# Three transposes of the compressed branch moved from the compression stage into the in-projection

## What is computed

```
proj = h @ w_in
chunks = kv_pad[:, :, :2].reshape(b, n_chunks, 16, 2, KV_HEADS, HEAD_DIM)
pa = einsum('bnlrkd,rlde->bnrke', chunks, w1[:, :16])
pb = einsum('bnlrkd,rlde->bnrke', chunks, w1[:, 16:])
hidden = gelu(pa[:, :-1] + pb[:, 1:] + pos_bias)
out = einsum('bnrke,ref->bnrkf', hidden, w2)      # r = 0: keys, r = 1: values
```

## Time and profile before

| what | value |
| --- | --- |
| median of 3 runs | 2507.48 us (2502.42 to 2513.97) |
| profiled execution | 2507.33 us, span 2505.7 us |
| mean granted TensorE clock | 0.939 of full |
| PE busy | 2372.7 us (95%) |
| DVE busy | 1292.7 us (52%) |
| ACT busy | 647.6 us (26%) |
| POOL busy | 188.6 us (8%) |
| in-projection of layer 0 ends, compression begins | at about 170 us |
| the same in layer 3 | at about 1958 us |

### The profile page before, as it was taken

How to read it: one execution, slowest core, us unless ns; L and a number is a source line. 1 busy time by engine, 2 the same in 40 slices (tenths; PEclk the granted TensorE clock), 3 DMA queues, 4 the chain that set the end, 5 groups by cost and what they waited for, 6 DMA issues and landing times. The chain is left out here.

```text
span 2505.7 us, 45103 instructions
## 1 busy us (share of the span) xinstructions
PE 2372.7 (95%) x18686; PEld 2002.1 (80%) x18686; DVE 1292.7 (52%) x2074; ACT 647.6 (26%) x1603; POOL 188.6 (8%) x346
## 2 busy tenths in 40 slices
PE   8999998899999888999999999999999998989998
PEld 6568765699987767999888856799996787648998
DVE  2237674366552383665443277076551686526565
ACT  1101372211022342210232195122011115522200
POOL 0245000000000010000000011000005520000000
PEclk8999898999999978999999857999999898999999
DMA  9886727956644318566534244666563675393440
GB/s 347 273 251 166 227 81 244 354 209 225 243 154 153 101 50 295 202 241 231 179 133 138 71 118 146 238 255 227 212 214 110 179 223 163 96 308 135 169 168 18
DMA packets 295776, 472.72 MB, mean 189 GB/s; under 512 B 22428, under 2 KB 120749, under 8 KB 295094
## 3 DMA queue, kind: packets, MB, share of 16 engines
q1 hardware_dynamic: 265714, 432.98, 50.7%
q0 software_dynamic: 10240, 20.99, 3.1%
q10 hardware_dynamic: 19618, 15.86, 2.1%
HBM read 448.72 MB, written 38.04 MB: 194 GB/s over the span
## 5 line engine op out<-in xcount | busy, mean ns | idle before, releaser
L632 PE MATMUL PS<-hT,ring 128*128 128x132 f32 x2048 | 249.6, 277 | 6.8 <-DVE hT L757 4.2
L632 PEld LDWEIGHTS PS<-hT,ring 128*128 128x128 f32 x2048 | 238.3, 190 | 12.0 <-issue 11.3
L632 PE MATMUL PS<-mT,arena 128*128 128x132 f32 x1536 | 184.6, 276 | 0.0
L632 PEld LDWEIGHTS PS<-mT,arena 128*128 128x128 f32 x1536 | 178.7, 190 | 0.0
L2688 PE MATMUL PS<-hT,ring 128*128 128x264 f32 x768 | 172.7, 386 | 0.1
L2688 PEld LDWEIGHTS PS<-hT,ring 128*128 128x128 f32 x768 | 145.1, 190 | 24.9 <-issue 0.4
L769 DVE TENSOR_TENSOR arena<-arena,PS 128x264 f32<-128x264 f32 x224 | 89.6, 426 | 131.1 <-PE PS L632 129.9
L948 POOL DMA_DIRECT2D arena<-in_cache_nsa_kv x192 | 97.4, 507 | 493.2 <-issue 438.8
L632 PE MATMUL PS<-arena,ring 128*128 128x132 f32 x1024 | 126.9, 277 | 0.0
L632 PE MATMUL PS<-hT,arena 128*128 128x132 f32 x1024 | 125.7, 276 | 0.0
L632 PE MATMUL PS<-mT,ring 128*128 128x132 f32 x1024 | 125.7, 276 | 0.0
(11 more groups left out here) (502 smaller groups left out, 4346.0 us busy)
## 6 DMA issues: line engine op xcount, KB each, us to landing
arena<-in_w_ada SPq DMA_DIRECT2D x36, 2048.0 KB, 12.1
ring<-in_w_mlp_in SPq DMA_DIRECT2D x32, 2048.0 KB, 8.9
ring<-in_w_mlp_out SPq DMA_DIRECT2D x32, 2048.0 KB, 8.3
ring<-in_w_ada SPq DMA_DIRECT2D x12, 2048.0 KB, 18.3
ring<-in_ssd_w_in SPq DMA_DIRECT2D x12, 2048.0 KB, 8.0
ring<-in_nsa_w_in SPq DMA_DIRECT2D x10, 2048.0 KB, 9.0
ring<-in_cache_nsa_kv SPq DMA_DIRECT2D x128, 128.0 KB, 3.7
ring<-in_hg_w_in SPq DMA_DIRECT2D x8, 2048.0 KB, 7.9
```

Of the source, the lines that this page charges most:

```text
L632: ins = nc.tensor.matmul(PS[:, bank, at:at + HALF], lhs[:, k, p * 128:(p + 1) * 128], rhs[:, k, :], start=opens and k == 0, stop=closes an ...
```

## The change

Transposes 1, 2 and 3 of the first cached round leave the compression stage. DVE makes them in the in-projection of each NSA layer, into the same place in the arena. In layer 0 DVE first waits for both stores of the bias matrices, and in both layers for all of POOL's pages of group 0; the three stand ahead of `move(10)` in layer 0 and ahead of the key copies. Transpose 0 stays where it was, since its quarter holds `wg`. In the compression stage the counts of the semaphore `turned` are adapted, and the differences 1, 2 and 3 no longer wait for it.

```diff
+        def rows_of(buffer, r, j):
+            return buffer.rearrange("p (y t) (r k h d) -> p t r h k y d", t=2, r=2, k=KV, h=2)[:, j // 2, r, j % 2]
+        def columns_of(x, j):
+            return x[:, j, :].rearrange("p (o b y) -> p y o b", o=4, b=2)
+        EARLY = (1, 2, 3)
...
             G = compress_buffers(P)
+            tokens = Place(P.at)(4, 1024)
             wg = P(8, 48)
...
                 if first:
+                    v.wait_ge(bias_kept.sem, bias_kept.at(32))
+                v.wait_ge(fetched_pool[0].sem, fetched_pool[0].at(1024))
+                for j in EARLY:
+                    turned.on(nc.vector.transpose(columns_of(tokens, j), rows_of(G[0], 0, j)))
+                if first:
                     move(10)
                     add(10)
                     move(11)
...
+            def turned_to(m):
+                return turned.at(1 if m in (0, *EARLY) else m + 1 - len(EARLY))
...
-                        sp.wait_ge(turned.sem, turned.at(8 * (g - 1)))
+                        sp.wait_ge(turned.sem, turned_to(8 * (g - 1) - 1))
...
                         j = m % 4
-                        v.wait_ge(turned.sem, turned.at(m + 1))
+                        if m not in EARLY:
+                            v.wait_ge(turned.sem, turned_to(m))
                         differed.on(nc.vector.tensor_tensor(delta[:, j, :].rearrange("p (a n) -> p a n", a=2), shifted(j),
...
                     turn(0)
                     sum_weights(0)
-                    turn(1)
                     position(0)
                     for m in range(1, last):
                         n, j = divmod(m, 4)
-                        if m + 1 < last:
+                        if m + 1 < last and m + 1 not in EARLY:
                             turn(m + 1)
```

More of the change, by code:

```diff
@@ L1285, in compressed @@
                 out_taken.on(ins)
[L1287 to L1295, removed]
             def shifted(j):
@@ L1317, in _ @@
                     for g in (2, 3):
-                        sp.wait_ge(turned.sem, turned.at(8 * (g - 1)))
+                        sp.wait_ge(turned.sem, turned_to(8 * (g - 1) - 1))
                         quarter_pages(sp, mybir.EngineType.SP, fetched, L, g, G, 0)
                     sp.wait_ge(bias_near.sem, bias_near.at(32))
-                    sp.wait_ge(turned.sem, turned.at(24))
+                    sp.wait_ge(turned.sem, turned_to(23))
                     src = kv_p[L, 0].rearrange("(c i t) r k d -> i c t (r k d)", i=4, t=2)
@@ L1332, in _ @@
                         if g > 1:
-                            gp.wait_ge(turned.sem, turned.at(8 * (g - 1)))
+                            gp.wait_ge(turned.sem, turned_to(8 * (g - 1) - 1))
                         quarter_pages(gp, mybir.EngineType.Pool, fetched_pool, L, g, G, 1)
@@ L1428, in _ @@
                                 else:
-                                    pe.wait_ge(turned.sem, turned.at(4 * n + j + 1))
+                                    pe.wait_ge(turned.sem, turned_to(4 * n + j))
                                 product_made.on(cached_product(n, j))
                             else:
-                                pe.wait_ge(turned.sem, turned.at(4 * n + j + 1))
+                                pe.wait_ge(turned.sem, turned_to(4 * n + j))
                                 product_made.on(prompt_product(n, j))
@@ L1460, in turn @@
                         if n < cached:
-                            ins = nc.vector.transpose(columns_of(j), rows_of(G[g % 2], r, j))
+                            ins = nc.vector.transpose(columns_of(x, j), rows_of(G[g % 2], r, j))
                         else:
```

## The result

| | before | changed |
| --- | --- | --- |
| median | 2506.43 us (20 runs) | 2512.70 us (20 runs) |
| spread | 2497.66 to 2515.81 | 2505.43 to 2523.45 |
| ratio | | 1.0025, 95% interval 1.0014 to 1.0036 |

The changed kernel is 6.3 us slower by the medians. It is a small loss, but it is clear of zero. The forecast was 2513.4 us, +6.0.

The account below looks back on a forecast made before the run. PE bounds the kernel, with layer 0's in-projection held by the load of unit 11. Late pages add 5.9 + 0.1 = +6.0 us there, the other parts 0: 2513.4 us forecast, range 2505 to 2520.

Parts of the forecast that it names:

- Landing of the pages: Layer 0's in-projection: POOL's last page starts at 153.17, lands 8.4 us later at 161.57, and ends DVE's waits.
- What stands behind the wait: Layer 0: `move(10)` queues behind DVE's wait, so PE stands at `turn(10)` until 167.35; unit 11's product starts +5.9 us.
- The product at the lower clock: Layer 0, product of unit 11: 3.62 us at clock 0.50, at most 0.2 more after longer idling; 0.1 taken.
- Zero in layer 3's in-projection: Three added transposes there cost 0, since DVE's idle time leaves 17 us of cover.
- Zero in the compression: Both layers: three transposes less save DVE some 5.4 us but bring PE 0; bounds -5.4 per layer and 0.
- The prediction's own sign of being wrong: The compression shrinking by over 2 us from start to end would refute the zero there.
- the wait of 2.5 us: Layer 0's compression: PE's 2.50 us wait at 229.83 for group 2's pages shifts with the stage and stays.
- DVE's lead is worth nothing: Compression, both layers: PE never waits for a moved transpose, so DVE being further ahead brings 0.
- A: Rival, layer 0: pages land before 155.7, transposes hide in idle time, 2507.5 us; chance 0.14 including in-between values.
- point of decision: Rival A's one deciding place: whether POOL's last page in layer 0 lands before 155.7.
- C: Rival: clock stays low longer, key transposes +2.2, first compression product +3.9, 2.5 given back; 2517 us; chance 0.12.
- B: Rival: differences pace PE in rounds 0 and 1, so both layers give up to 5.4 us; 2502.7; chance 0.06.

Follow-up runs that it names:

- layer 0 only: Changed kernel with transposes 1 to 3 early in layer 0 alone, layer 3 as before: 2512.89 us, ratio 1.0028.
- shared pages: Earlier page issue, and POOL issues a quarter of SP's group 1 pages: changed kernel 2499.11 us, 0.9976; kernel before 2497.60 us, 0.9971.
- without constants: Pages issued earlier and split with POOL, PE's ten opening matmuls on constants omitted: transposes moved 2503.01 us, 0.9980; not moved 2497.82 us, 0.9961.
- earlier pages: POOL issues group 0's second half behind the sixth unit, not the eighth: changed kernel 2501.23 us, 0.9981; kernel before 2503.80 us, 0.9990.

## Why the prediction was right

*Landing of the pages* (161.57, 7.3 us behind the gates' start): 7.18 measured, ended by the pages as said. It was read off the transfer's own row and not off layer 3's 2.2 us, which would have given zero.

*What stands behind the wait*: `turn(10)` at 12.73 us behind the gates' start (13.1 forecast), product of unit 11 at 13.14 (13.3), idle time 8.18 (8.5). Shown by doubling the work (+6.43) and by moving the wait two instructions on (-5.1). One of the reasons given for the landing was read with a wrong label: the shares of 52.2% and 49.8% are those of 158 to 159 us and not of 155 to 160, where it was 49.3% for the pages and 53.5% for the weights. The argument stands by either.

*The product at the lower clock*: 3.64 us against 3.62; I had given it 0.1 more and it took nothing. What I missed is the instruction behind it. The key transposes took 2.49 us and not 2.16, since the clock was still low. The sum came out by small errors that cancel, which is luck: the product starts 5.73 us later and not 5.9, the product takes 0.1 less than allowed, and the key transposes take 0.33 more. The prediction also says that the clock fell in the idle time before the product of unit 11. The trace of the kernel before has 1.00 for that idle time (159.1 to 161.6 us); the clock fell at about 161.8, when the product had begun.

*Zero in layer 3's in-projection*: shown, with 17.9 us of cover where 17 were forecast, and by the 47.28 us that stay.

*Zero in the compression*: right to within what was measured. Over the profiled executions with pages unshared, the six compressions without moved transposes average 123.98 us (122.62 to 124.65) and the ten with them 123.37 (122.27 to 124.09). 0.6 us a layer may be there, but the spread of one kernel's two layers is larger. The prediction's own sign of being wrong, a compression over 2 us shorter, did come in layer 3 (124.49 to 122.37). It does not speak against the zero, since layer 3 of the kernel "layer 0 only", where nothing is moved, has 122.62. The rows give the reason: the compression before waits 2.33 us in round 3, and PE then takes 4.38 us from the product behind the wait to the start of round 4; the changed kernel waits 1.31 and the other 1.73, and both take 2.70.

The forecast that the wait of 2.5 us would stay was off: it was 1.64 in layer 0 and 1.31 in layer 3 (2.50 and 2.33 before). In layer 0 an earlier landing, 56.2 us behind the start of the stage and not 56.8, gives 0.5 of it, and PE coming 0.35 later to round 2 the rest. In layer 3 it is the landing alone (56.0 and not 56.9). Why the pages landed earlier stays open. The reason given, that pages and PE's own work and not DVE pace the stage, is shown by the shared pages (1.4 to 4.6 us a layer off) and by the equal lengths without constants. "DVE's lead is worth nothing" is true of the length of the stage; PE's round 0 gains half a microsecond from it without the constants, and PE then waits that much longer for pages.

*The rivals*: A did not come true, by the very row that spoke against it, but its point of decision held. With pages landed before the bias store the cost vanished. That the weights of unit 11 would then be on time as well was no part of it. Of C a small part came: 0.33 us of the 2.2 on the key transposes, and 0.34 on the first product of layer 0's compression (its position term of round 1 starts 16.67 us behind the start of the stage, 16.33 before), which the wait for group 2 took back. B is answered above, at the kernels without constants.

## What to carry to other kernels

Work moved into another engine's idle time costs nothing only where the data is there at that moment. Look up when its last transfer lands, and put the wait behind every instruction that someone else waits for; here two instructions made five of six microseconds. Before moving work off an engine, look for one wait on it. A margin of half a microsecond is no wait, and making it six brought the length of this stage nothing; where it did turn into a wait, the wait was as small as the margin, and the next transfer swallowed it. The gain lay in the transfers: a few pages out of the way of the weights, and a fairer split of the issuing between two queues, without the moved transposes (0.9971), or with the constants left out too (0.9961). The intervals of these two overlap, so no run here says which is the better.

## What the runs showed of the hardware

The granted clock can fall while PE is busy. In the kernel before with earlier pages PE never idled from 150 to 162 us, and yet (windows: us, busy and count of PE, PEld, DVE, ACT, POOL, then PEclk, DMA share, GB/s):

```profile
153.00:156.00 3.00, 3.00 (x37) 2.80 (x29) 0.29 (x1) 1.02 (x1) 0.00 (x0) 1.00 0.80 314
156.00:158.00 2.00, 2.00 (x25) 1.95 (x24) 0.00 (x0) 0.00 (x0) 0.00 (x0) 0.76 0.92 306
158.00:160.00 2.00, 2.00 (x33) 1.53 (x34) 0.20 (x1) 0.33 (x2) 0.00 (x0) 0.50 0.10 34
```

It fell to 0.50, 1.2 GHz, in the gates, whose 48 instructions have 48 columns each. They took 5.06 us there and 4.55 where it did not fall, and the product of unit 11 2.83 against 1.95 in the changed kernel with earlier pages. That is 1.4 of the 1.5 us between 12.93 and 11.40. It is not the transposes that decide it. Of the six kernels with earlier pages it fell in the gates in three (5.06 us unmoved, and with shared pages 5.13 unmoved and 5.24 moved), and not in the other three (moved, and the two without constants). In the changed kernel it fell while PE idled, and was at 0.50 until 169 us, with the product of unit 11 under way since 165.83:

```profile
160.00:163.00 3.00, 0.00 (x0) 0.00 (x0) 3.00 (x2) 0.00 (x0) 0.00 (x0) 0.51 0.77 302
...
167.00:169.00 2.00, 2.00 (x44) 1.82 (x40) 0.00 (x0) 0.00 (x0) 0.00 (x0) 0.50 0.03 8
169.00:171.00 2.00, 2.00 (x20) 1.05 (x10) 0.93 (x4) 0.00 (x0) 0.00 (x0) 0.67 0.00 0
```

The key transposes, at 169.40, were the ones that paid for it.

Time that the edits leave alone moves by more than this change is worth: the stretch of some 1655 us from the end of layer 0's compression to layer 3's gates differed by 10 us between profiled executions, though the part of it that the edits reach, layer 3's in-projection, took the same 47.28 us in each. A single pair of executions can't show six microseconds; the distances inside the stage can.
